# One-hot first visit, first norm by row block, split up products for fifteen experts

## What is computed

```python
u = rms_norm(h, ln_w); parts = split(u @ w_in)      # first block
h = h + concat(y_conv, y_mla, y_ret) @ w_out
x = x + merged @ w_out_2                            # second block
hf = rmsnorm(x, g_ffn)
expert_id, share = two best of 16, by group and then by expert
hid = silu(hf @ w_gate[e]) * (hf @ w_up[e])         # 1024 to 256
x = x + sum over the two experts of share * (hid @ w_down[e])
```

## Time and profile before

| | |
|---|---|
| time of the runs | 1452.06 us median of 3 (1451.78 to 1453.04) |
| profiled execution | 1451.33 us, its span 1449.4 us |
| granted clock, mean | 0.965 of full speed |
| busy share | PE 92%, DVE 39%, ACT 37%, POOL 28% |
| DMA in the span | 179.60 MB, mean 124 GB/s |

### The profile page before, as it was taken

The page is one execution under the profiler, slowest core; times in us unless marked ns, Lnnn a source line. Parts: engine busy times, 40 slices in busy tenths (PEclk is TensorE's granted clock), DMA queues, the critical chain, the costliest instruction groups (busy, mean ns, idle before and its releaser), DMA issues.

```text
span 1449.4 us, 16277 instructions
## 1 busy us (share of the span) xinstructions
PE 1326.3 (92%) x6144; PEld 982.7 (68%) x6144; DVE 563.8 (39%) x1294; ACT 539.9 (37%) x952; POOL 408.4 (28%) x203
## 2 busy tenths in 40 slices
PE   3999989889899999999998999999899996899996
PEld 3788666457678766765877777888787785444443
DVE  2164353534320135236897453234423315121225
ACT  4353434343542447445333554323433333111111
POOL 3255221014555222233423112543115322000002
PEclk9999999979999999999999999999999997899999
DMA  4232434013444221221322112432034605989915
GB/s 146 65 102 75 158 103 132 17 52 124 139 126 160 73 58 59 59 73 46 114 66 94 45 45 66 163 106 73 8 147 129 250 27 205 384 318 371 331 59 190
DMA packets 76474, 179.60 MB, mean 124 GB/s; under 512 B 11217, under 2 KB 22791, under 8 KB 69735
## 3 DMA queue, kind: packets, MB, share of 16 engines
q1 hardware_dynamic: 68656, 165.48, 33.7%
q0 software_dynamic: 2624, 8.41, 1.6%
q10 hardware_dynamic: 5110, 4.62, 1.1%
HBM read 153.32 MB, written 25.17 MB: 123 GB/s over the span
## 4 chain that ended last, share of the span: by engine, by line
PE 43%; DVE 8%; ACT 2%; issue 1%; DMA 1%; POOL 0%; DVEq 0%; ACTq 0%
PE ps L993 8%; PE ps L1477 8%; PE ps L995 8%; PE ps L994 8%; PE ps L1484 4%; DVE work L2551 1%; PE ps L1371 1%; PE ps L1354 1%; DVE dq L2560 1%; DVE best L2549 1%; PE ps L1470 1%; PE ps L1327 1%; DVE mix_lo L2330 1%; PE ps L1399 1%; PE ps L1361 1%
## 5 line engine op out<-in xcount | busy, mean ns | idle before, releaser
L877 POOL TENSOR_TENSOR w_lo<-raw,w_hi 128x1024 fp32r<-128x1024 f32 (+1 forms) x158 | 377.7, 2407 | 786.2 <-ACT w_hi L1691 786.2
L993 PE MATMUL ps<-w_hi,act_hi 128*128 128x512 f32 (+1 forms) x560 | 234.7, 419 | 6.9 <-POOL w_lo L877 3.6
L1691 ACT ACTIVATE w_hi<-raw 128x1024 fp32r<-128x1024 f32 (+1 forms) x158 | 158.9, 1033 | 169.3 <-PE ps L995 160.7
L994 PE MATMUL ps<-w_lo,act_hi 128*128 128x512 f32 (+1 forms) x560 | 220.3, 393 | 0.0
L995 PE MATMUL ps<-w_hi,act_lo 128*128 128x512 f32 (+1 forms) x560 | 219.6, 392 | 0.0
L993 PE MATMUL ps<-w_hi,mix_hi 128*128 128x512 f32 x320 | 131.8, 412 | 9.9 <-DVE mix_lo L2330 6.4
L993 PEld LDWEIGHTS ps<-w_hi,act_hi 128*128 128x128 f32 (+1 forms) x560 | 105.0, 187 | 47.2 <-issue 13.8
L995 PE MATMUL ps<-w_hi,mix_lo 128*128 128x512 f32 x320 | 126.3, 395 | 0.0
L994 PE MATMUL ps<-w_lo,mix_hi 128*128 128x512 f32 x320 | 126.2, 394 | 0.0
L995 PEld LDWEIGHTS ps<-w_hi,act_lo 128*128 128x128 f32 (+1 forms) x560 | 104.8, 187 | 25.4
L994 PEld LDWEIGHTS ps<-w_lo,act_hi 128*128 128x128 f32 (+1 forms) x560 | 105.0, 188 | 24.0 <-issue 1.5
(11 more groups left out here) (447 smaller groups left out, 1925.4 us busy)
## 6 DMA issues: line engine op xcount, KB each, us to landing
raw<-in_w_in SPq DMA_DIRECT2D x92, 512.0 KB, 3.5
gu<-in_w_gate SPq DMA_DIRECT2D x16, 1024.0 KB, 6.1
...
```

Source lines behind the costliest of these rows:

```text
L877: pool.tensor_tensor(lo[:, 0:a], raw[:, g % RAW_SLOTS, 0:a], hi[:, 0:a].bitcast(F32), ALU.subtract).then_inc(*POOL.done(("w_lo", g)))
L993: pe.matmul(dst, l_hi, r_hi, start=start, stop=False, skip_group_check=skip)
L994: pe.matmul(dst, l_hi, r_lo, start=False, stop=False, skip_group_check=skip)
L1691: nc.scalar.activation(split_slot(g)[0][:, 0:a], raw[:, g % RAW_SLOTS, 0:a], ACTF.Copy).then_inc(*ACT.done(("w_hi", g)))
```

## The change

**First norm.** SP loads the meta tokens first, gives each block of 128 rows its own semaphore and puts the gain of this norm and the identity between the first blocks; five constants go behind the first four weight loads (`late_constants`). The scales are made in two halves (`first_scale(0)` for rows 0 to 255, `first_scale(1)` for the rest and the meta tokens), two weight units are split before the first turns (`first_split`), chunks 0 to 3 are turned block by block (`first_turn`), chunks 4 to 7 one at a time between parts of `latent`, which waits for its own two chunks only. The other gains are turned after the first unit (`constants`).

**First visit.** The first expert visited is number 1 (`FIRST_E`; number 0 comes second). Its turned rows come from products of `xs_ffn` with one-hot matrices that DVE makes in `place` (`x_hot(t)`, 8 plain float32 matmuls for each of four row blocks), added up in two banks. Its rows are not read back. `r_weights`, the counts for the overflow flag and the one-hot matrices of the last experts (`last_oh` on DVE, `last_hot`) move behind the first visits.

**Up products.** Visits 1 to 15 take rounded and remainder operands: ACT rounds each of 8 chunks of gate and up weights with the gain to `e_hi`, DVE writes the remainder over the landed weights (`gu_lo`), ACT and DVE do the same with the turned rows (`x_hi`, `x_lo`), and PE issues 24 matmuls by `product`. There is one `e_hi`: its chunks 2u and 2u + 1 are rewritten when PE has passed them (`up_part`). Weights land in five sets. `yg` and other tiles move in SBUF.

```diff
-E_SETS = 6
+E_SETS = 5
+FIRST_E = 1
...
-    order = [("constants",), ("norm", "h")]
-    order += item("latent") + [("latent_sums",)] + item("k_rope") + [("mla_tables",)]
+    order = [("first_gain",), ("first_scale", 0), ("first_scale", 1), ("first_split",), ("first_turn",)]
+    lat = item("latent")
+    order += [("first_chunk", 0), ("first_chunk", 1), ("turn_chunk", 4), lat[0], ("first_chunk", 2), ("turn_chunk", 5), lat[1]]
+    order += [("first_chunk", 3), ("turn_chunk", 6), ("first_meta",), ("first_chunk", 4), lat[2]]
+    order += [("constants",), ("turn_chunk", 7), ("first_chunk", 5), ("first_chunk", 6), ("first_chunk", 7)]
+    order += lat[3:] + [("latent_sums",)] + item("k_rope") + [("mla_tables",)]
...
-    order += [("r_turn", 3), ("route", 1, 1), ("rank", 1), ("pos", 1), ("r_stat", 3), ("r_logits", 3), ("route", 2), ("rank", 2), ("pos", 2)]
-    order += [("r_weights",), ("last_hot", 0), ("over_flag",), ("x_turn", 0)]
+    order += [("r_turn", 3), ("x_hot", 0), ("route", 1, 1), ("rank", 1), ("pos", 1), ("r_stat", 3), ("r_logits", 3)]
+    order += [("x_hot", 1), ("x_hot", 2), ("route", 2), ("rank", 2), ("pos", 2), ("x_hot", 3), ("counts",), ("x_turn", 0)]
+    order += [("split", 1, 0), ("r_weights",)]
     for e in range(N_EXP):
-        order += [("up", e)] + [("x_turn", e + 1)] * (e + 1 < N_EXP) + [("down", e - 1)] * (e > 0) + [("turn", e)]
-        if e == 2:
-            order += [("last_hot", 1)]
+        ahead = [("split", e + 1, u) for u in range(e == 0, 4)] if e + 1 < N_EXP else []
+        order += ahead[:-1] + [("up", e)] + [("x_turn", e + 1)] * (e + 1 < N_EXP) + ahead[-1:] + [("down", e - 1)] * (e > 0) + [("turn", e)]
+        order += [("over_flag",)] * (e == 0) + [("last_hot", e - 1)] * (1 <= e <= 2) + [("last_oh", e)] * (e < 2)
...
-            for e in range(X_BUFS):
-                sp.dma_start(xe[:, e, :], expert_rows(x_rows, e)).then_inc(xe_in[e], 16)
-            for e in (4, 5):
-                load_up(sp, e, e, gu_in[e])
-                load_down(sp, e, e, dn_in[e])
+            for e in range(1, X_BUFS + 1):
+                sp.dma_start(xe[:, e % X_BUFS, :], expert_rows(x_rows, expert_of(e))).then_inc(xe_in[e % X_BUFS], 16)
+            sp.wait_ge(*PE.after("xT", 0, 1))
+            load_up(sp, 4, 4, gu_in[4])
+            load_down(sp, 4, 4, dn_in[4])
...
+            def x_hot(t):
+
+                if t == 0:
+                    for half in range(2):
+                        claim(half, (DVE, ("xeT", 0, half)))
+                pe.wait_ge(*ACT.after("xs_ffn", t))
+                pe.wait_ge(*DVE.after("hot", t))
+                for k in range(KC):
+                    mm = pe.matmul(ps[:, k // 4, P * (k % 4):P * (k % 4) + P], xs_ffn[:, t, P * k:P * k + P], oh[t // 2][:, t % 2, :],
+                                   start=(t == 0 and k % 4 == 0), stop=(t == NT - 1), skip_group_check=True)
+                    if t == NT - 1 and k % 4 == 3:
+                        mm.then_inc(*PE.done(("xT", 0, k // 4)))
...
-                for half in range(2):
-                    pe.wait_ge(*DVE.after("xeT", e, half))
-                up_product(2 + e % 2, e % E_SETS, e % 2).then_inc(*PE.done(("up", e)))
+                if e == 0:
+                    up_product(2, 0, e).then_inc(*PE.done(("up", e)))
+                    return
+                for k in range(KC):
+                    if k % 4 == 0:
+                        pe.wait_ge(*DVE.after("xeT", e, k // 4))
+                    pe.wait_ge(*DVE.after("e_lo", e, k))
+                    mm = product(ps[:, 2 + e % 2, :], x_hi[:, k, :], x_lo[:, k, :], e_hi[:, k, :, :], gu_lo[e % E_SETS][:, :, k, :],
+                                 k == 0, k == KC - 1)
+                    if k % 2:
+                        mm.then_inc(*PE.done(*([("up_part", e, k // 2)] + [("up", e)] * (k == KC - 1))))
...
+            def split(e, u):
+                s = e % E_SETS
+                if u == 0:
+                    act.wait_ge(gu_in[s], 32 * (e // E_SETS + 1))
+                    if e == 1:
+                        act.wait_ge(*PE.after("acc", "w_out21", NT - 1))
+                if e > 1:
+                    act.wait_ge(*PE.after("up_part", e - 1, u))
+                for k in (2 * u, 2 * u + 1):
+                    nc.scalar.activation(e_hi[:, k, :, :], gu[s][:, :, k, :], ACTF.Copy,
+                                         scale=g8[:, k:k + 1]).then_inc(*ACT.done(("e_hi", e, k)))
...
+                for k in (2 * u, 2 * u + 1):
+                    dve.wait_ge(*ACT.after("e_hi", e, k))
+                    dve.scalar_tensor_tensor(gu_lo[s][:, :, k, :], gu[s][:, :, k, :], g8[:, k:k + 1], e_hi[:, k, :, :].bitcast(F32), ALU.mult,
+                                             ALU.subtract).then_inc(*DVE.done(("e_lo", e, k)))
```

More of the change, by code:

```diff
@@ L503, in program @@
         xe = sb("xe", [P, X_BUFS, D], 81)
-        xeT = sb("xeT", [P, 2, KC, P], 93)
+        xeT = sb("xeT", [P, KC, P], 93)
+        x_hi = sb("x_hi", [P, KC, P], 93, F32R)
+        x_lo = sb("x_lo", [P, KC, P], 97, F32R)
+        e_hi = sb("e_hi", [P, KC, 2, D_EXP], 24, F32R)
         ye = sb("ye", [P, 2, D], 101)
@@ L1057, in part @@
                     return
+                if name == "latent" and u == 0 and b == 2:
+                    pe.wait_ge(*DVE.after("meta_lo", "h"))
                 if u == 0:
@@ L1472, in x_turn, with up_product @@
                         tr.then_inc(*PE.done(("xT", e, k // 4)))
-            def up_product(bank, s, i):
+            def up_product(bank, s, turned=None):
                 for k in range(KC):
-                    mm = pe.matmul(ps[:, bank, :], xeT[:, i, k, :], gu[s][:, :, k, :], start=(k == 0), stop=(k == KC - 1))
+                    if turned is not None and k % 4 == 0:
+                        pe.wait_ge(*DVE.after("xeT", turned, k // 4))
+                    mm = pe.matmul(ps[:, bank, :], xeT[:, k, :], gu[s][:, :, k, :], start=(k == 0), stop=(k == KC - 1))
                 return mm
@@ L1658, in _ @@
                     rank_rows(*a)
+                elif step == "counts":
+                    counts()
+                elif step == "x_hot":
+                    x_hot(*a)
                 elif step == "x_turn":
@@ L2721, in place @@
                 link(dve.tensor_tensor(r_at[:, a:b, :], r_hot[:, a:b, :], r_at[:, a:b, :], ALU.mult))
+                dve.wait_ge(*DVE.after("first_slots"))
+                for t in ts:
+                    dve.tensor_scalar(oh[t // 2][:, t % 2, :], first_slots[:, :], r_at[:, t, FIRST_E:FIRST_E + 1], None,
+                                      ALU.is_equal).then_inc(*DVE.done(("hot", t)))
                 link(dve.tensor_reduce(rt[:, 13, a:b], r_one[:, a:b, :], X, ALU.add))
@@ L2785, in x_turn @@
                     dve.wait_ge(*PE.after("xT", e, half))
-                    if e >= 2:
-                        dve.wait_ge(*PE.after("up", e - 2))
-                    x_turned(e % 2, half).then_inc(*DVE.done(("xeT", e, half)))
+                    if e == 0:
+                        x_turned(half).then_inc(*DVE.done(("xeT", e, half)))
+                        continue
+                    rows = slice(4 * half, 4 * half + 4)
+                    dve.wait_ge(*ACT.after("x_hi", e, half))
+                    dve.scalar_tensor_tensor(x_lo[:, rows, :], ps[:, half, :].rearrange("p (k n) -> p k n", k=4), 1.0,
+                                             x_hi[:, rows, :].bitcast(F32), ALU.mult, ALU.subtract).then_inc(*DVE.done(("xeT", e, half)))
             def up(e):
```

223 lines of the change are left out of this document (163 added, 60 removed).

## The result

The changed kernel takes 1410.93 us (median of 4 runs, 1408.12 to 1414.84) beside 1452.55 us (median of 4) for the kernel before: ratio 0.9712, 95% interval 0.9685 to 0.9739. The forecast was 1410.5. The forecast column adds up to 41.5: this profiled execution is 2.3 us above its median, so its parts fall short of what the median shows.

A forecast was written before the change was run, and what follows sets the result against it. PE, busy 92% of the span, was taken as the bound, plus places where it idles. Gains 19.4 + 12.7 + 8.0 + 1.4 = 41.5 off 1451.33 give 1409.8, with 0.73 for the median 1410.5 us; forecast 1406 to 1413, range 1402 to 1422.

The forecast's parts named there:

- Visits: Expert visits 1 to 15: split up products cut the period from 11.39 to 10.02 us, gain 19.4 us.
- plus 2.35 each: Among the visits: each of two one-hot turns of the last experts adds 2.35 us to the fourteen periods.
- First norm: Start of the kernel: first product at 16.9 us, stage end at 41.2, gain 8.0 us (5 to 11).
- First visit: Hand-over to the experts: first up product at about 1227.4 instead of 1237.75, gain 12.7 us (10 to 14.5).
- The end: After the last up product's start: only its shorter product counts, gain 1.4 us (0 to 1.6).
- Five landing sets: Up weight loads, five sets instead of six: 36 us of lead, no cost taken, 0 to 5 us for the range.
- Rival B: Experts: the transfers set the pace, 1413 to 1425 us, typical 1416; chance 12%.
- Rival C: Visits: ACT or DVE feeds PE late by about 0.6 us each, 9 us in all, 1419; chance 8%.
- D: Start: something behind the latent stage still ends at its old time, losing the 8 us, 1418.5; chance 8%.
- E: More gain: full clock at the hand-over (2 us), front at its best (3), nothing lost, 1405; chance 11%.
- F: DVE in each visit: e_lo costs 1.28 us, DVE needs 13.5 us a visit and bounds it, 1460; chance 3%.
- G: Hand-over still waits for the scattered rows, first visit gives 3 us instead of 12.7, 1420; chance 3%.

The follow-up runs named there:

- e1: The changed kernel once more, unedited, with six runs: 1409.67 us, ratio 0.9698 to the kernel before.
- e6: Changed kernel plus two more remainders of 512 elements on DVE per visit, into a tile nobody reads: 1416.48 us.
- e5: Changed kernel with POOL starting its first w_lo only when DVE has scaled all tiles and the meta tokens: 1409.64 us, ratio 0.9707.
- e2: Changed kernel with the first norm back as a whole, ahead of the latent projection, weights split behind it: 1413.82 us.
- e3: Changed kernel with the first visit's rows read back from DRAM and turned, instead of one-hot products: 1422.40 us.
- e11: Changed kernel plus 18 identity turns filling PE's two gaps ahead of the last one-hot products: 1409.65 us, ratio 0.9706.
- e4: Changed kernel with plain float32 up products in all sixteen visits, nothing split, five landing sets kept: 1432.49 us.
- e8: Changed kernel with four landing sets for the up weights instead of five: 1410.34 us, ratio 0.9697.
- e7: Changed kernel plus eight more remainders of 512 elements on DVE per visit, into a tile nobody reads: 1463.62 us, ratio 1.0087.

## Why the prediction was right

The mechanisms of the four parts were right in the main, and the total, 1410.5, was met by 0.4 us; so close a hit is in part luck. In the profile compared above the terms were off by -2.1, -1.3, +1.6 and -1.7 us and give 38.0 instead of 41.5. The median came out right because that execution lies 2.3 us above it, where the forecast allowed 0.7. e1's profile of the same program gives 7.5, 13.1, 20.9 and 1.4, which is 42.9: how far the clock falls at the hand-over, in the tail and in the middle decides on more than the terms were off by.

**Visits, 19.4 forecast, 21.0 found.** The period was right: 10.02 and 10.01 us, from products 0.227 us apart. The term mis-sized was that of the one-hot turns of the last experts, "plus 2.35 each": visits with such a turn take 11.7, so it costs 1.7. (The prediction's 4.9 us for these turns before is 164.45 - 159.46 = 5.0.) Feeding was right: e_lo 746 ns in the group and issued every 0.66 to 0.68 us (0.7 assumed), e_hi 717 (at most 685 assumed, a little over), DVE 7.7 (8.8 assumed). The cover inside a steady visit was 1.8 us and not 1.2 (the second x_lo done at 8.2, forecast 8.8), and e6's two remainders left 1.1 of it; the smallest cover was at a place for which the prediction worked out none, the turn of the last experts.

**First norm, 8.0 forecast, 5.5 found at latent_sums, 5.9 at the routing.** The steps that failed are "two scalings of 2.74 / 4 give 13.8" and "Two w_lo of 1.79 (7.17 / 4) are ready at 16.2 if POOL is undisturbed": POOL and DVE hold each other up, and PE waits for DVE's side. The prediction named this and left it out of its sum. e5 takes it away and lands at 17.47 and 41.01 against the forecast's 16.9 and 41.2. A smaller part is the second tile of x, for which ACT waits 1.17 us. e2 puts 4.5 us on the row blocks and leaves 1.7 to what stands around them. The 0.4 us between the two marks are less than the middle varies.

**First visit, 12.7 forecast, 11.4 found** (13.1 in e1). Less the front's 5.9, the first up product starts at 1228.3 where 1227.4 was forecast: x_hot(3) and the counts at the lower clock. The low clock was seen as a possibility ("1.7 at the full clock and 3.5 at the half one"); the counts behind x_hot(3), 1.7 us at the lower clock, were left out. e3 puts 9.5 us on the one-hot products and 1.9 on the steps moved away, which the forecast did not tell apart. The price of the lower clock here is in e11: 25.18 with the gaps filled, 27.91 without.

**The end, 1.4 forecast, -0.3 found.** The shorter product does gain: e4's tail against e1's is 34.54 - 33.19 = 1.35. In the profiled execution the clock fell in the last down product and took 1.7 back, which the forecast had not looked for; in e1's profile it did not, and the tail gains 1.4.

**Five landing sets, 0 forecast, 0 found** (e4, and even four in e8). Rival B, the transfers, fell with them: share 1.02 and no wait. Rival C, late feeding, did not occur. D fell as a mechanism: the end of the stage moved with its start; that the start gave 2 us less has another reason. E, 1405, was not reached: the fastest execution of this program took 1408.12. F's mechanism was shown by e7 with two remainders, 1.32 us, in place of one: slower than before, as it said; the 745 ns of yl_lo was the right row to judge by. G fell: the first visit does not wait for the scattered rows.
